# A hybrid decoder layer on one core: where the value steps of paged attention stand among the slots

## What is computed

```python
def sb_block(q, k, v, bias, q_pos, k_pos):
    z = jnp.einsum('bhqd,bhkd->bhqk', q, k) * (SB_HEAD_DIM ** -0.5)
    z = z + bias[None, :, None, None]
    mask = k_pos[None, :] < q_pos[:, None]
    log_beta = jax.nn.log_sigmoid(z)
    log_keep = jnp.where(mask, jax.nn.log_sigmoid(-z), 0.0)
    tail = lax.cumsum(log_keep, axis=3, reverse=True) - log_keep
    a = jnp.where(mask, jnp.exp(log_beta + tail), 0.0)
    return jnp.einsum('bhqk,bhkd->bhqd', a, v)

# token mixing: one projection -> [stick-breaking attention | gated linear attention] -> norms -> one projection
proj = h @ w_in
# samples: keys and values of 1024 past tokens from a pool of pages
k_past = cache_k[l][page_table].reshape(dec_b, -1, SB_HEADS, SB_HEAD_DIM)
v_past = cache_v[l][page_table].reshape(dec_b, -1, SB_HEADS, SB_HEAD_DIM)
out = jnp.concatenate([o_sb, o_g], axis=-1) @ w_out
# then x = x + gate * norm(out), and a SwiGLU feed-forward sub-layer of the same form
```

## Time and profile before

| | |
|---|---|
| runs | 1492.05, 1495.88, 1499.24 us |
| the profiled execution's own time | 1496.05 us |
| its span | 1494.3 us |
| TensorE busy with matmuls | 1428.4 us (96%) |
| VectorE, ScalarE, GpSimd busy | 921.6, 665.5, 103.8 us |
| data read from HBM | 382.28 MB |
| granted TensorE clock, mean | 0.983 |

### The profile page before, as it was taken

The page is one execution under the profiler, slowest core; times in us unless marked ns, Lnnn a source line. Parts: engine busy times, 40 slices in busy tenths (PEclk is TensorE's granted clock), DMA queues, the critical chain, the costliest instruction groups (busy, mean ns, idle before and its releaser), DMA issues.

```text
span 1494.3 us, 29193 instructions
## 1 busy us (share of the span) xinstructions
PE 1428.4 (96%) x11238; PEld 1273.0 (85%) x11238; DVE 921.6 (62%) x1519; ACT 665.5 (45%) x1303; POOL 103.8 (7%) x200
## 2 busy tenths in 40 slices
PE   6779999998899999998999999999999999999997
PEld 2247787887667777796899999999999999999997
DVE  2243588995777666368756766567665675446444
ACT  1023477777656454345543434434344343334333
POOL 0000311113322210000000000000000000200000
PEclk9979999999899999999999999999999999999999
DMA  9999999999999979985755565555655555855552
GB/s 370 422 343 364 390 391 405 374 352 391 396 370 343 340 255 356 409 307 225 250 182 183 170 193 173 181 182 170 191 174 181 182 170 192 231 181 181 181 178 95
DMA packets 139330, 396.82 MB, mean 266 GB/s; under 512 B 13162, under 2 KB 17681, under 8 KB 126433
## 3 DMA queue, kind: packets, MB, share of 16 engines
q1 hardware_dynamic: 118018, 319.66, 61.3%
q0 software_dynamic: 21232, 76.10, 13.4%
HBM read 382.28 MB, written 11.34 MB: 263 GB/s over the span
## 4 chain that ended last, share of the span: by engine, by line
PE 83%; DMA 11%; DVE 2%; ACT 2%; issue 1%; POOLq 0%; SPq 0%; POOL 0%; DVEq 0%; ACTq 0%
PE ps L1981 24%; PE ps L1982 24%; PE ps L1983 24%; DMA ada_s<-in_w_ada 5%; PE ps L1915 4%; DMA v_page<-in_cache_v 3%; PE ps L2113 2%; DMA ada_r<-in_w_ada 1%; PE ps L2039 1%; DMA raw<-in_w_ffn_gate 1%; DMA k_page<-in_cache_k 1%; ACT k_page L803 1%; DMA k_page<-in_cache_v 1%; ACT w_hi L715 0%; PE ps L2141 0%
## 5 line engine op out<-in xcount | busy, mean ns | idle before, releaser
L1981 PE MATMUL ps<-h_hi,w_hi 128*128 128x264 f32 x2304 | 667.8, 290 | 11.0 <-DVE h_lo L1249 3.6
L1982 PE MATMUL ps<-h_lo,w_hi 128*128 128x264 f32 x2304 | 659.2, 286 | 0.0
L1983 PE MATMUL ps<-h_hi,w_lo 128*128 128x264 f32 x2304 | 658.6, 286 | 0.0
L1981 PEld LDWEIGHTS ps<-h_hi,w_hi 128*128 128x128 f32 x2304 | 438.9, 190 | 55.8 <-issue 34.9
L1806 DVE TENSOR_TENSOR w_lo<-raw,w_hi 128x1024 fp32r<-128x1024 f32 x254 | 307.2, 1214 | 273.1 <-ACT w_hi L1047 271.7
L1047 ACT ACTIVATE w_hi<-raw 128x1024 fp32r<-128x1024 f32 x264 | 278.5, 1059 | 408.2 <-PE ps L1983 384.4
L1982 PEld LDWEIGHTS ps<-h_lo,w_hi 128*128 128x128 f32 x2304 | 438.2, 190 | 0.5
L1983 PEld LDWEIGHTS ps<-h_hi,w_lo 128*128 128x128 f32 x2304 | 436.9, 190 | 0.0
L1261 DVE TENSOR_TENSOR w_lo<-raw,w_hi 128x1024 fp32r<-128x1024 f32 x138 | 168.7, 1223 | 145.9 <-ACT w_hi L715 145.5
L715 ACT ACTIVATE w_hi<-raw 128x1024 fp32r<-128x1024 f32 x128 | 135.1, 1056 | 172.5 <-PE ps L1983 155.1
L1982 PE MATMUL ps<-act_lo,w_hi 128*128 (+1 forms) x704 | 200.4, 285 | 0.0
(11 more groups left out here) (362 smaller groups left out, 1213.8 us busy)
## 6 DMA issues: line engine op xcount, KB each, us to landing
ada_r<-in_w_ada SPq DMA_DIRECT2D x64, 1024.0 KB, 9.1
raw<-in_w_in SPq DMA_DIRECT2D x96, 512.0 KB, 8.3
raw<-in_w_ffn_gate SPq DMA_DIRECT2D x88, 512.0 KB, 3.5
raw<-in_w_ffn_up SPq DMA_DIRECT2D x88, 512.0 KB, 4.4
raw<-in_w_ffn_down SPq DMA_DIRECT2D x88, 512.0 KB, 4.6
ada_s<-in_w_ada SPq DMA_DIRECT2D x32, 1024.0 KB, 13.7
k_page<-in_cache_k POOLq DMA_DIRECT2D x64, 512.0 KB, 8.0
v_page<-in_cache_v POOLq DMA_DIRECT2D x38, 512.0 KB, 8.4
```

Source lines behind the costliest of these rows:

```text
L1981: mm(out, w_hi, xh, start=first, stop=False)
L1982: mm(out, w_hi, xl, start=False, stop=False)
L1983: return mm(out, w_lo, xh, start=False, stop=last)
```

## The change

It touches the order of side work in slots 56 to 92 and what hangs on it. Steps 0 to 5 go to every second slot, or nearly (56, 58, 61, 63, 65, 67), steps 6 to 15 to slots 69 to 78, one each; steps 16 to 31 go to slots 81 to 92, with two steps in each of the slots 83, 85, 87 and 89. The number of instructions is the same. The switch of four of the value pages' buffers to those of the key pages comes at page 25 instead of page 32. `dec_rows`, `dec_probs` and `dec_select` of samples 0 to 3 and 4 to 7 move from slots 75 and 76 to slot 79, `put_rows` from 76 to 80, and the transposes go into bank 7 instead of bank 5.

```diff
+        V_PLACE = [VPA[m % 5] if m < 25 else VPB[m % 5] for m in range(TS * PAGES)]
...
-        AV_SLOT = [56, 57] + [60 + 14 * i // 13 for i in range(14)] + [77 + i for i in range(16)]
-        AV_AT = {s: v for v, s in enumerate(AV_SLOT)}
+        AV_SLOT = [56, 58, 61, 63, 65, 67] + [69 + i for i in range(10)] + [81, 82, 83, 83, 84, 85, 85, 86, 87, 87, 88, 89, 89, 90, 91, 92]
+        AV_AT = {s: [v for v in range(32) if AV_SLOT[v] == s] for s in AV_SLOT}
...
-        DROW_AT = {75: 0, 93: 1}
+        DROW_AT = {79: 0, 93: 1}
...
-                if m == 32:
+                if m == 25:
                     pool.wait_ge(k_even, 32)
                     pool.wait_ge(k_odd, 32)
...
-                if s in AV_AT:
-                    for m in (2 * AV_AT[s] + 5, 2 * AV_AT[s] + 6):
+                for v in AV_AT.get(s, ()):
+                    for m in (2 * v + 5, 2 * v + 6):
                         if m < TS * PAGES:
                             v_page(m)
...
                 if g == 9:
-                    act.wait_ge(av_used, 16)
+                    act.wait_ge(av_used, 12)
...
-                if st == 76:
-                    for b in range(4, 8):
-                        dec_probs(b)
...
                     dec_rows(DROW_AT[st])
+                if st == 79:
+                    for b in range(4, 8):
+                        dec_probs(b)
...
-                if st == 76:
+                if st == 80:
                     put_rows(0)
...
                 elif v == 16:
-                    pe.wait_ge(dout_ready, 1)
+                    pe.wait_ge(d_put, 1)
...
                 if h == 0:
-                    pe.wait_ge(d_put, 1)
+                    pe.wait_ge(kt_ready, 1)
...
-                if st in AV_AT:
-                    page_values(AV_AT[st])
+                for v in AV_AT.get(st, ()):
+                    page_values(v)
...
-                if st == 75:
-                    pe.wait_ge(kt_ready, 1)
-                    dec_select(0, 5)
+                if st == 79:
+                    dec_select(0, 7)
```

More of the change, by code:

```diff
@@ L591, in v_page @@
                 page = pool.value_load(PT[0:1, m:m + 1], min_val=0, max_val=NPOOL - 1)
-                pool.dma_start((VPA if m < 32 else VPB)[m % 5][:, :],
+                pool.dma_start(V_PLACE[m][:, :],
                                pool_v[bass.ds(page, 1), :, :].rearrange("o p n -> p (o n)")).then_inc(vpage_in[m % 5], 16)
@@ L1440, in put_rows @@
                 even, odd = (bass.AP(tensor=src.tensor, offset=src.offset, ap=[src.ap[0], [36, 2], [P + 1, 4], [H, 4]])
-                             for src in (ps[:, 5 if x == 0 else 7, 0:512], ps[:, 5 if x == 0 else 7, 64:512]))
+                             for src in (ps[:, 7, 0:512], ps[:, 7, 64:512]))
                 link(v.tensor_copy(dst, even))
@@ L2108, in page_values @@
                 elif v == 16:
-                    pe.wait_ge(dout_ready, 1)
+                    pe.wait_ge(d_put, 1)
                 for j in range(4):
                     m = 2 * v + j // 2
-                    page = (VPA if m < 32 else VPB)[m % 5][:, j % 2 * 512:j % 2 * 512 + 512]
+                    page = V_PLACE[m][:, j % 2 * 512:j % 2 * 512 + 512]
                     ins = mm(ps[32 * j:32 * j + 32, 7, :], AD[:, b % 4, 2 * pair + j // 2, :], page,
```

## The result

The changed kernel takes 1506.54 us in the median of five runs (1503.54 to 1507.58), the kernel before 1495.88 in the runs beside it. The ratio is 1.0071, its 95% interval 1.0055 to 1.0088: slower, by 10.7 us. The forecast was 1504.0. The profiled execution took 1506.54 us, its span is 1504.7.

The account below looks back on a forecast made before the run. TensorE, busy 96%, was taken as the bound, its idle time in value-page waits. Removing 12.2 and 5.3 us and adding 6.0, 1.3, 1.0, 1.5 and 15.8 gave +8.1: 1504.0 us against 1495.88, range 1487 to 1512.

Parts of the forecast that it names:

- Removed waits: Slots 56 to 79: TensorE's 12.2 us of waits for value pages go, with 5.3 us of low clock behind them.
- Key pages: Slots 62, 63 and 68: TensorE waits 6.0 us for VectorE's late key pages; one low-clock stretch adds 1.3 us.
- 2.35: Slots 62 and 63: TensorE's wait behind key pages taken as 2.35 us, less than slot 68's 3.65.
- Steps 6 to 15: One value step in each slot leaves slightly too little time for pages: +1.0 us, bounds 0 and 3.5.
- Slots 79 and 80: ScalarE's copy and `a_dec` delay unit 80 by 0.7 us and head 1's softplus by 0.8: +1.5 us.
- The doubled slots: Four pairs, 83/84 to 89/90: two steps in one slot leave value pages late, 3.95 us a pair, +15.8 us.
- the formula: Cost per pair of slots: time from step v-2's end to page 2v+1's landing, 8.3 us, less 4.35.
- leave the traffic what it was: Doubled slots: 331 GB/s before and requests slowed by waits keep traffic unchanged, so the median landing of 7.0 us was taken.
- Unit 80: Starts some 12.5 us sooner than before: 4 us for four steps then behind it, 8.5 net from earlier slots.
- Rival (b): Faster: spread-out requests land in 4.8 us throughout, no key page is late, 1487 us; chance 0.18.
- Rival (c): No change: landing some 6 us, a pair costs 2.95, slot 68 waits 0.75, no clock term, 1493 us; chance 0.27.
- The estimate of 3.2 us for a page: A 512 KB transfer asked for by GpSimd takes 2.0 us plus bytes by 436 GB/s; a pair would cost 0.2 us.

Follow-up runs that it names:

- run 11: Changed kernel with key pages 50 to 53 and 55 to 63 copying one eighth of their columns: 1497.78 us, 1.002 of the kernel before.
- run 6: Changed kernel with only GpSimd's requests reordered, value pages 4 to 14 asked for later: 1504.75 us, 1.0074 of the kernel before.
- run 1: Kernel before with only steps 16 to 31 moved to the change's slots: 1509.14 us, 1.0099 of the kernel before.
- run 2: Changed kernel with a sixth value page buffer for pages 37 to 48: 1500.03 us, 1.0025 of the kernel before.
- run 4: Changed kernel with value pages 37 to 63 copying one eighth of their columns: 1494.27 us, 0.999 of the kernel before.
- run 9: Changed kernel with late steps spread over half slots, five buffers kept: 1497.93 us, 1.0019 of the kernel before.
- run 3: Changed kernel with a sixth key page buffer from page 52 on: 1502.14 us, 1.0036 of the kernel before.
- run 5: Changed kernel with both a sixth value page and a sixth key page buffer: 1497.27 us, 1.0016 of the kernel before.
- run 12: Fastest kernel (both sixth buffers, reordered requests, late steps at half slots) with step 2 and page 9's request one slot later: 1495.73 us.

## Why the prediction was right, and where it was not

**Removed waits, -12.2 and -5.3.** The waits of steps 1 to 5 are gone, as said. The low clock was sized wrong, on both sides of the sum. The prediction took the loss in the 24 products of one unit for the whole, but step and head work stand between the wait and those products, and they ran at the lower clock too. From the end of each wait to the end of those 24 products the traces of before have 5.61, 6.65, 5.56 and 5.54 us at a mean granted clock of 0.70, 0.56, 0.69 and 0.69. The shares missing there make 8.0 us, not 5.3.

**Key pages, +6.0 and +1.3 predicted; 10.0 and 4.3 measured.** The mechanism and both places were right: TensorE waits in slots 63 (4.6) and 68 (4.8) for VectorE, and run 11 takes them to 2.7 and 1.1 by making key pages small. The sizes were too low for two reasons. In slot 68 I took a landing of 8.9 us. Page 62 was asked for at 394.34 and landed at 405.55, 11.2 us; TensorE was 0.8 us later than computed and POOL 0.65 quicker, which leaves 4.8 for 3.65. Ten pages less did not mean a lower rate there: units 56 to 69 got 9.2 us shorter and move 400 GB/s, 398 before. In slot 63 I took 2.35 "since the first pages come before the slots have sped up". That step of the prediction failed: 4.6 us were measured. Key page 50 is asked for at 354.0 and 354.3 us and lands at 365.7 and 366.1 in the two kernels. It is the same page at the same time, but VectorE waits 5.9 us for it now (run 6 shows the row, and that the wait in slot 63 falls to 2.0 us when this page lands 5 us sooner). It had waited 1.1 in the kernel before, from its timeline:

```profile
365.74 0.29 DVE L1312 SCALAR_TENSOR_TENSOR k_page<-k_page,q_bcast 128x128 f32<-128x128 f32 x1 [1.06 <-DMA k_page<-in_cache_k]
```

The low clock: the 24 products behind the two waits have a clock of 0.76 and 0.62 and take 1.0 and 1.4 us over 3.02. Counted from the end of each wait, as above, it is 6.57 us at 0.65 and 5.03 us at 0.60, and 4.3 us are lost.

**Steps 6 to 15, +1.0; measured 2.6**, within its bounds of 0 and 3.5: steps 9, 10 and 15 wait 1.2, 0.2 and 1.3.

**Slots 79 and 80, +1.5; measured 0.** No wait stands there in the trace of after beyond those that were there before. What I costed was ScalarE's and VectorE's lateness; that other work of TensorE covered it is argued, no run tries it.

**The doubled slots, +15.8; measured 13.4.** This was the term that decided, and runs 1, 2, 4 and 9 all bear out its mechanism: moving only these steps costs 13.2 us, a sixth buffer gives back 7.1, pages of 64 KB 11.4, and even spacing alone takes half the waits away. The size is 2.4 too high, as far as the formula goes because pages landed in 6.3 us, not 7.0. That the waits "leave the traffic what it was" was wrong: 283 GB/s are moved there in place of 331. With 6.3 the same formula gives 4 x (7.6 - 4.35) = 13.0. The four pairs were not alike, though, with waits of 4.2, 3.4, 0.6 and 2.4 us. The pair 85/86 has the low clock right behind its wait, and a slow stretch is time in which the ring of the next pair can catch up; that this is what makes 87/88 so small is argued, not tried. So 13.0 against 13.4 is partly luck: the formula takes four equal pairs. What the time consists of can be added up: TensorE waits 10.5 us, 10.2 more than before, and from the ends of the two longest waits the clock costs 3.2 us (7.18 us at a mean of 0.79, 7.70 at 0.78), 13.4 in all.

**Unit 80, forecast 12.5 us sooner, came 5.9 sooner.** One part is a plain miscount: three steps stand behind it that stood before it (19 against 16), not four. Then come the key pages' 5.1 us too little (with 2.4 for their clock), the 1.6 of steps 9 to 15 and 0.5 from the later start of unit 56, less the 0.7 of slot 79 that didn't come: 7.5 with the step, of 6.6 to be explained. Of the 0.9 us gained beyond that 0.8 are the clock's: it gave back 8.0 and took 4.3, 3.7 us net, where 5.3 and 2.4 in the products alone had made 2.9.

**The sum.** Too low were the key pages by 4.0, their clock by 3.0 and steps 6 to 15 by 1.6; too high were the removed clock, which gave 2.7 us more, slots 79 and 80 by 1.5 and the doubled slots by 2.4. That is 8.6 against 6.6, so 8.1 becomes 10.1; with the 0.5 us before unit 56 it is 10.6, and measured were 10.7 by the medians and 10.4 by the profiled executions. The sign and the deciding term were right by their mechanism. That 1504.0 lies within 2.5 us of 1506.54 is luck: errors of 7 to 9 us stand on both sides. Rival (b) is out: the shortest landing of the late stretch is 3.8 us, but the median 6.3. Rival (c) had that landing, about right, and failed on the key pages, which it put at 1.5 us with no clock. The estimate of 3.2 us for a page, by the Trainium skill's page "DMA: Bandwidth & Descriptors" (Anatomy of one DMA, SWDGE path), was again not met: no page of the late stretch lands in under 3.8 us. Smaller pages do land sooner, in 2.9 us with 64 KB against 6.3 with 512 KB in the same slots (run 4), but the DMA engines also move 132 GB/s there in place of 283, so no run here separates the part by bytes from the traffic.

**What stays open**: why the gains of runs 2 and 3 add only in part (run 5), why the profile of run 9 shows half of its gain, and why the pair 87/88 waits so little.

## What to carry to other kernels

With a ring of n buffers, compare the time from a buffer's last use to the landing of what comes next with the spacing of the uses, not with their mean rate: two uses side by side halve the spacing, and spreading them at half slots gave 8 us back here with the same buffers, although TensorE's own work grew by some 1.6 us. Before a wait is removed, look up which engine waits in its cover and for which transfer: the 1.1 us that VectorE waited for key page 50 became 5.9 when TensorE stopped being late. A wait taken away by order alone brought nothing in run 6 and again nothing in run 12, since others came up behind it; a further buffer brought 4 to 7 us (runs 2 and 3). And count the low clock from the end of the wait, whatever work stands there, not only in the products that are easy to compare.

## What the runs showed of the hardware

A sixth page in flight raised the key pages' landing from 9.5 to 11.1 us in the median, in a stretch (355 to 420 us) that moved 376 GB/s without it and 398 with it, and still paid. Pages of 64 KB landed in 2.9 us in run 4, where the DMA engines were busy at a share of 0.45 (489 to 526 us), but in 5.2 us in run 11 at a share of 0.94 (355 to 420 us), 1.8 times as long for the same bytes. Behind the changed kernel's waits of 2.6, 3.4, 4.6 and 4.8 us the granted clock was the lower one for a part of what followed; behind its waits of 1.5 us (steps 19 and 28) it stayed at 1.00. Behind the two long late waits it was over before the next unit began: the products of units 85 and 87 ran at 1.00 (501.89 to 504.90 and 518.41 to 521.50 us), and the loss lay in the step and the head work ahead of them.
